# Twenty projection blocks beside a state space scan as three reduced-precision products, with the weights' low parts made by accumulating DMAs

## The chip, the cores and the metric

The kernel runs on one core of a Trainium2 chip. The metric is device time in microseconds (us) of one launch. Five engines work side by side and meet only through semaphores: TensorE (PE, matrix products), VectorE (DVE), ScalarE (ACT), GpSimd (POOL) and SyncE (SP, which only issues DMAs here).

## The reference

Two blocks are computed on 256 tokens of width 1024. The first has two layers (a gated delta rule with attention, then a convolution layer, each followed by a feed-forward part). The second is one hybrid layer, and only its beginning is touched:

```python
def hybrid_layer(x, g_pre_mix, w_in, ...):
    h = rmsnorm(x, g_pre_mix)
    proj = jnp.einsum('bld,dn->bln', h, w_in)          # 1024 -> 6664 columns
    (u_s5, x_conv, b_conv, c_conv, q, k, v, f_logit, gate_logits) = jnp.split(proj, offsets, axis=-1)
    y_a = s5_mixer(u_s5, ...)                          # state space scan, 32 groups of 16 channels, 64 states
    y_b = short_conv_mixer(x_conv, b_conv, c_conv, conv_w)
    y_c = forgetting_attention(q, k, v, f_logit, b_f)
    gates = jax.nn.sigmoid(gate_logits + b_gate)
    merged = sum of gates[i] * (y_i @ w_branch_i)
    x = x + rmsnorm(merged @ w_out, g_post_mix)
    ...                                                # feed-forward part with relu squared
```

`s5_mixer` multiplies u by a complex input matrix, runs a linear recurrence with a complex diagonal over the tokens, multiplies by a complex output matrix and applies gelu and a gate. Everything is float32.

## The kernel before

**Projections.** The product with `w_in` is cut in blocks of 128 output columns. `BLOCKS3` lists 52 of them in order: `in_a` (12 blocks, numbers 0 to 11: u, q, k), `in_v` (4, numbers 12 to 15), `in_b` (12, numbers 16 to 27: the convolution's inputs) and `in_g` (24, numbers 28 to 51: the gates). A plain block is eight float32 matmuls of 128x128 weights on 256 tokens (`feature_block`). ACT copies the finished block out of PSUM (blocks take turns in banks 0 and 1). The gate blocks from `GATE0` = 9 on are made in another way: both operands are split into a high part, rounded to float32r, and a low part, the rest. A block is then 24 float32r matmuls (high by high, low by high, high by low, lines L1456 to L1458). ACT rounds the weights (`gate_round`), DVE subtracts (`gate_split`).

**Weights** come in chunks of three blocks into `ring`, four slots that SP fills as soon as the last block of a slot's chunk before is done.

**The scan** has `S5T` = 16 steps on DVE, each of 128 complex states. Step i waits for its phase table from POOL (`s5_tab`, made by `tables(i)`) and for its input product from PE (`s5_in`, two steps at a time), and then runs L2935 to L2958. POOL's `tables(i)` waits for the rotation of step i-2 (`s5_n`), since it writes that step's buffer. PE takes the states out with `s5_out`, two steps at a time.

**The order beside the scan is written out by hand.** The generator `projections` exists once on PE and once on ACT, and both take `next(filler)` at the same places: four blocks ahead of the scan, then one or two blocks a step (`BESIDE`). PE runs `s5_in(i // 2 + 1)` after the first block of an even step, `s5_out(i // 2 - 1)` at the end of an odd step from 3 on, and `cum_k(i - 13)` in steps 13 to 15. `FORGET` puts small pieces of the attention's forget gate after DVE's steps 7, 9, 11, 14 and 15. `forget(0)` (L2889, L2890) makes `logf_in`, for which ACT waits in its own step 8 (`act.wait_ge(logf_in, 1)`). `forget(3)` (L2908, L2909) reads `cum_k(0)` out of bank 7, so that `cum_k(1)` (L1477) can be written there.

**The gates' input.** ACT rounds `gate_x` (the normalised tokens) to `gate_x_hi` in steps 10 to 13, one of four pairs a step. DVE subtracts after the scan (`gate_x_lo`).

Of the kernel before, what the change touches and what calls it, by code (L numbers as in the profile page):

```python
# [23 lines left out]
F32 = mybir.dt.float32  # L24
# [321 lines left out]

BLOCKS3 = [(_name, _b) for _name, _n in (("in_a", 12), ("in_v", 4), ("in_b", 12), ("in_g", 24)) for _b in range(_n)]
GATE0, GATES = 9, 24
BESIDE = [1 if _i in (2, 5, 8) else 2 for _i in range(S5T)]
FORGET = {7: 0, 9: 1, 11: 2, 14: 3, 15: 4}  # L350

# [13 lines left out]
def build(nc, w, w_mod1, cols_in, rows_in, consts_in, b_out_in, c_bd_in, glu_in, b_in, x_in, ctx_in, out):  # L365
    ctx = ExitStack()
    w = {**w, "mod1": w_mod1}
    with ctx:
# [265 lines left out]
        gates_ready, merged = sem("gates_ready"), sem("merged")  # L634
        gate_x_rounded, gate_x_split = sem("gate_x_rounded"), sem("gate_x_split")
        gate_w_hi, gate_w_lo = sem("gate_w_hi"), sem("gate_w_lo")
        hyb_o_w_hi, hyb_o_w_lo, mix_hi, mix_lo = sem("hyb_o_w_hi"), sem("hyb_o_w_lo"), sem("mix_hi"), sem("mix_lo")
        merged_hi, merged_lo = sem("merged_hi"), sem("merged_lo")
        out2_w_hi, out2_w_lo = sem("out2_w_hi"), sem("out2_w_lo")
# [12 lines left out]
        y_a, y_b = yT[:, 0:4, :], yT[:, 4:8, :]  # L652
        mT, m_lo, m_hi = view(tok_t, 0, KT, T), view(tok_r, 0, KT, T), view(aT_r, 0, KT, T)
        gate_x, gate_x_hi, gate_x_lo = aT[:, :, 0:T], view(aT_r, 0, KT, 2 * T)[:, :, T:2 * T], view(tok_r, 0, KT, T)
        gate_hi = [diag_r[:, 0:D], rowbc_r[:, 0:D], arena_r[:, 14376:14376 + D], z_r[:, 0:D]]
        out2_hi = [arena_r[:, at:at + D] for at in (1024, 4096, 14376, 0, 2048, 3072, 5120, 6144)]
        bT = view(tok_t, 0, 2, 4, P)
# [117 lines left out]
        def _(pe):  # L775
# [659 lines left out]
            def projections():  # L1435

                for name, b in BLOCKS3:
# [11 lines left out]
                    elif name == "in_g" and b >= GATE0:  # L1449
                        w_lo_b, w_hi_b = gate_weights(b, ring_r)  # L1450
                        if b == GATE0:
                            pe.wait_ge(gate_x_split, 4)
                        pe.wait_ge(gate_w_lo, b - GATE0 + 1)
                        for k in range(KT):
                            at = slice(k * P, k * P + P)
                            mm(bank(use)[:, 0:T], w_hi_b[:, at], gate_x_hi[:, k, :], start=(k == 0), stop=False)  # L1456
                            mm(bank(use)[:, 0:T], w_lo_b[:, at], gate_x_hi[:, k, :], start=False, stop=False)  # L1457
                            last = mm(bank(use)[:, 0:T], w_hi_b[:, at], gate_x_lo[:, k, :], start=False, stop=(k == KT - 1))  # L1458
                        filled(last, use)
                    else:  # L1460
                        filled(feature_block(use, slot(c)[:, (b % 3) * D:(b % 3 + 1) * D], lambda k: aT[:, k, 0:T],
                                             fresh=(5,) if (name, b) == ("in_a", 0) else ()), use)
# [153 lines left out]
        def _(act):  # L1616
# [508 lines left out]
            def projections():  # L2125

                for name, b in BLOCKS3:
# [12 lines left out]
                    if name == "in_g" and GATE0 <= b < GATES - 4:  # L2140
                        gate_round(b + 4)
                    yield

            def gate_round(b):

# [1 line left out]
                act.wait_ge(ring_ready[SLOT_OF[c]], 16 * (TURN_OF[c] + 1))  # L2147
                fn(rounded, raw, ACT.Copy).then_inc(gate_w_hi, 1)

            filler = projections()  # L2150
            for _ in range(4):
                next(filler)
            for n, use in enumerate(USE["b_bar"]):
# [13 lines left out]
            for i in range(S5T):  # L2167
# [7 lines left out]
                if i == 8:  # L2175
                    act.wait_ge(logf_in, 1)
                    ch(fn(lf_a, lf_a, ACT.Exp, scale=-1.0))
                    fn(lf_a, lf_a, ACT.Ln, bias=1.0).then_inc(logf_sp, 1)
                if 10 <= i < 14:
                    pair = slice(2 * (i - 10), 2 * (i - 10) + 2)  # L2180
                    fn(gate_x_hi[:, pair, :], gate_x[:, pair, :], ACT.Copy).then_inc(gate_x_rounded, 1)
            next(filler)
            act.wait_ge(s5_state, S5T)
            for b in range(GATE0, GATE0 + 3):
# [69 lines left out]
        def _(dve):  # L2254
# [626 lines left out]

            norm_scale(5)
            norm_evac(5)

            def forget(step):
                if step == 0:
# [202 lines left out]
        def _(pool):  # L3089
# [103 lines left out]
            def tables(i):  # L3193
# [12 lines left out]
                        ch(last)  # L3206
                last.then_inc(s5_tab, 1)

            for i in range(S5T):
                if i >= 2:  # L3210
                    pool.wait_ge(s5_n, i - 1)
                tables(i)
# [115 lines left out]
```

## Time and profile before

| | |
|---|---|
| median of 3 runs | 1311.59 us (1310.51 to 1314.21) |
| the profiled execution | 1312.18 us |
| its span, first to last instruction | 1310.3 us |
| mean granted TensorE clock | 0.985 |
| busy: PE, DVE, ACT, POOL | 1246.6, 908.5, 542.9, 125.2 us |

The profile is one execution. A timeline row is a group of like instructions in order of time: start, length, engine, line, operation, output and inputs, count, and in brackets the idle time before it with what ended it. A float32 matmul stands as two instructions, so 16 of L841 are one block.

### The profile page before, as it was taken

How to read it: one execution, taken by the hardware profiler on the slowest of the kernel's cores; microseconds unless marked ns; L12 is line 12 of the kernel's file. 1: busy time of each engine (PE TensorE's matmuls, PEld its weight loads, DVE VectorE, ACT ScalarE, POOL GpSimd, SP SyncE). 2: the span in 40 equal slices, each digit the busy share in tenths (PEclk: the TensorE clock that was granted, in tenths of full speed). 3: DMA queues.
4: the chain of work that ended last, by engine and by line, in shares of the span. 5: the costliest groups of instructions: out<-in, count | busy, mean ns of one | idle time of the engine just before them, and what ended most of it. 6: DMA issues, size and time to landing. Idle time of an engine off the chain costs nothing. (4 is left out here: it accounts for less than half of the span.)

```text
span 1310.3 us, 19537 instructions
## 1 busy us (share of the span) xinstructions
PE 1246.6 (95%) x7388; PEld 992.4 (76%) x7388; DVE 908.5 (69%) x1557; ACT 542.9 (41%) x907; POOL 125.2 (10%) x165
## 2 busy tenths in 40 slices
PE   4999979999999999999899999899999999899997
PEld 1777646567888887874688888787878987788886
DVE  0548896568777775886777776399977445777776
ACT  2654256446334444014644444302236534544443
POOL 0052021000000002000000000255530000000000
PEclk8999979999999999999999999899999999999999
DMA  9322367865655555422555555124233323555551
GB/s 389 139 86 97 137 267 292 331 269 206 236 192 188 185 182 192 146 80 69 196 206 180 183 187 204 60 86 179 106 134 128 143 104 125 188 192 192 186 182 50
DMA packets 24950, 225.80 MB, mean 172 GB/s; under 512 B 2737, under 2 KB 2865, under 8 KB 4658
## 3 DMA queue, kind: packets, MB, share of 16 engines
q1 hardware_dynamic: 23328, 220.31, 45.9%
q10 hardware_dynamic: 1554, 4.56, 1.0%
q8 instruction: 46, 0.75, 0.2%
q14 instruction: 22, 0.18, 0.0%
HBM read 223.81 MB, written 1.05 MB: 172 GB/s over the span
## 5 line engine op out<-in xcount | busy, mean ns | idle before, releaser
L964 PE MATMUL psum<-aT_r,arena_r 128*128 128x512 f32 x920 | 327.5, 398 | 2.4 <-DVE arena_r L2382 1.9
L2382 DVE TENSOR_TENSOR arena_r<-ring,arena_r 128x1024 fp32r<-128x1024 f32 x188 | 220.4, 1221 | 97.9 <-ACT arena_r L1716 97.9
L965 PE MATMUL psum<-aT_r,arena_r 128*128 128x256 f32 x920 | 258.1, 281 | 0.0
L1716 ACT ACTIVATE arena_r<-ring 128x1024 fp32r<-128x1024 f32 x188 | 186.9, 1051 | 143.4 <-PE psum L999 133.0
L999 PE MATMUL psum<-arena_r 128*128 128x512 f32 x876 | 213.4, 392 | 0.0
L841 PE MATMUL psum<-aT,ring 128*128 128x256 f32 (+1 forms) x896 | 209.7, 393 | 0.0
L964 PEld LDWEIGHTS psum<-aT_r,arena_r 128*128 128x128 f32 x920 | 172.8, 188 | 44.9 <-issue 3.0
L841 PEld LDWEIGHTS psum<-aT,ring 128*128 128x128 f32 x896 | 169.3, 190 | 38.3 <-issue 17.2
L999 PEld LDWEIGHTS psum<-arena_r 128*128 128x128 f32 x876 | 159.5, 188 | 34.7
L965 PEld LDWEIGHTS psum<-aT_r,arena_r 128*128 128x128 f32 x920 | 173.7, 189 | 2.6
L1728 ACT ACTIVATE nrm<-nrm 128x256 f32<-128x256 f32 x76 | 31.8, 418 | 165.1 <-DVE nrm L2400 161.9
L824 PE MATMUL psum<-ring,cond 128*32 128x384 f32 x512 | 53.7, 548 | 20.6 <-DMA consts<-in_consts 12.5
L2770 DVE SCALAR_TENSOR_TENSOR arena<-arena,cols 128x256 f32<-128x256 f32 x120 | 52.8, 482 | 1.9
L824 PEld LDWEIGHTS psum<-ring,cond 128*32 128x32 f32 x512 | 14.9, 118 | 49.0 <-issue 36.9
L2400 DVE TENSOR_REDUCE nrm<-psum 128x256 f32<-128x512 f32 x73 | 49.8, 683 | 0.0
L2417 DVE TENSOR_TENSOR nrm<-nrm 128x256 f32<-128x256 f32 x76 | 32.4, 426 | 22.1 <-ACT nrm L1728 16.6
L2407 DVE TENSOR_REDUCE nrm<-psum 128x256 f32<-128x512 f32 x42 | 29.0, 691 | 20.8 <-PE psum L965 20.8
L2507 DVE SCALAR_TENSOR_TENSOR arena<-arena,cols 128x512 f32<-128x512 f32 (+1 forms) x48 | 35.3, 763 | 1.1
L1457 PE MATMUL psum<-aT_r,ring_r 128*128 128x256 f32 x120 | 33.8, 282 | 0.0
L2425 DVE TENSOR_TENSOR arena_r<-nrm,arena_r 128x256 fp32r<-128x256 f32 x73 | 31.1, 425 | 2.6 <-DVE arena_r L2423 0.2
L3188 POOL MEMSET arena<- 128x24 f32 x1 | 0.1, 121 | 311.6 <-DVE nrm L2309 311.6
L1560 PE MATMUL psum<-yT,ring 128*128 128x256 f32 x128 | 28.9, 379 | 0.0
(551 smaller groups left out, 1894.4 us busy)
## 6 DMA issues: line engine op xcount, KB each, us to landing
ring<-in_w_ffn SPq DMA_DIRECT2D x44, 1536.0 KB, 6.7
ring<-in_w_mod SPq DMA_DIRECT2D x32, 1536.0 KB, 8.6
ring<-in_w_ff SPq DMA_DIRECT2D x32, 1024.0 KB, 4.9
ring<-in_w_in_g SPq DMA_DIRECT2D x8, 1536.0 KB, 6.8
ring<-in_w_conf_i SPq DMA_DIRECT2D x8, 1024.0 KB, 4.8
ring<-in_w_hyb_f SPq DMA_DIRECT2D x4, 1536.0 KB, 6.7
ring<-in_w_in_a SPq DMA_DIRECT2D x4, 1536.0 KB, 6.5
ring<-in_w_in_b SPq DMA_DIRECT2D x4, 1536.0 KB, 6.3
```

Source lines behind the costliest of these rows:

```text
L824: last = mm(mod_banks[run][0][q:q + 32, :], cond[:, at:at + 32], slot(c)[:, k * MOD_C:(k + 1) * MOD_C], start=(m == m0 and k < 4), stop=(m ...
L841: last = mm(bank(use)[:, out_at:out_at + rhs(k).shape[1]], weights[:, k * P:(k + 1) * P], rhs(k), start=(k == 0), stop=(k == KT - 1))
L964: mm(bank(use).rearrange("p (a t) -> p a t", a=2), hi, x_both[:, :, k, :], start=(k == 0), stop=False)
L965: last = mm(bank(use)[:, T:2 * T], lo, x_hi[:, k, :], start=False, stop=(k == KT - 1))
L999: last = mm(Y[:, t, half * 512:half * 512 + 512], act_part, w_part[:, half * 512:half * 512 + 512], start=(isinstance(i, int) and j == 0 a ...
L1457: mm(bank(use)[:, 0:T], w_lo_b[:, at], gate_x_hi[:, k, :], start=False, stop=False)
L1716: fn(out_hi[2] if last_out else w_hi[j % 2][:, at], slot(c)[:, at], ACT.Copy).then_inc(split_hi, 1)
L2382: tt(lo, slot(c)[:, at], hi.bitcast(F32), ALU.subtract).then_inc(split_ready, 1)
L2400: summed = v.reduce_sum(g_sum[:, j % 2, :], bank(gate).rearrange("p (a t) -> p t a", a=2), axis=AXX)
L2417: tt(h_tmp, sg[:, j % 2, :], u_sum if parts == 3 else sg[:, j % 2, :], ALU.mult).then_inc(h_step, 1)
L2507: last = stt(cv[:, b, 0:n, :], cin[:, b, 0:n, k:k + T], taps[:, b, k:k + 1], cv[:, b, 0:n, :], ALU.mult, ALU.add)
L2770: last = stt(cc[:, c, :], cu[:, c, k:k + T], dww[:, c, k:k + 1], cc[:, c, :], ALU.mult, ALU.add)
```

## The change

Blocks 4 to 11 and 16 to 27 (`PARTED`, twenty of them) are made of three float32r products, as the late gate blocks are.

- ACT rounds `gate_x` ahead of the first block and no longer in steps 10 to 13. DVE makes a second low part of it, `scan_x_lo`, ahead of the scan. The later `gate_x_lo` stays.
- For each block ACT first writes the negated weights, rounded, to one of five buffers (`scan_negate`, five blocks ahead). POOL then issues a DMA that adds the weights to that buffer (`scan_add`), which leaves the weights less their rounded value there: the low part. When that DMA has landed, ACT rounds the weights in place in the ring (`scan_round`, two blocks ahead).
- ACT's two instructions follow the copy of a block in `projections`, after its `yield`. POOL issues the DMAs in its loop over the steps, ahead of the wait for `s5_n` and of `tables(i)`: five ahead of `tables(1)`, then 2, 1, 0, 1, 2, 2, 2, 2, 2, 1 ahead of `tables(2)` to `tables(11)`.
- PE waits for `scan_hi` ahead of each of the blocks.

```diff
+PARTED = [_n for _n, (_name, _b) in enumerate(BLOCKS3) if _name == "in_b" or _name == "in_a" and _b >= 4]
+PARTED_AHEAD = 5
...
+        scan_x_lo = view(decay_r, 0, KT, T)
+        scan_lo = [ybuf_r[:, 0:D], ybuf_r[:, D:2 * D], o_r[:, 0:D], arena_r[:, 12328:12328 + D], arena_r[:, 13352:13352 + D]]
...
+                    elif BLOCKS3.index((name, b)) in PARTED:
+                        s = PARTED.index(BLOCKS3.index((name, b)))
+                        w_hi_s, w_lo_s = scan_weights(s, ring_r), scan_lo[s % PARTED_AHEAD]
+                        if s == 0:
+                            pe.wait_ge(scan_x_split, 4)
+                        pe.wait_ge(scan_hi, s + 1)
+                        for k in range(KT):
+                            at = slice(k * P, k * P + P)
+                            mm(bank(use)[:, 0:T], w_hi_s[:, at], gate_x_hi[:, k, :], start=(k == 0), stop=False)
+                            mm(bank(use)[:, 0:T], w_lo_s[:, at], gate_x_hi[:, k, :], start=False, stop=False)
+                            last = mm(bank(use)[:, 0:T], w_hi_s[:, at], scan_x_lo[:, k, :], start=False, stop=(k == KT - 1))
+                        filled(last, use)
...
                     yield
+                    n = BLOCKS3.index((name, b))
+                    if n + 2 in PARTED:
+                        scan_round(PARTED.index(n + 2))
+                    if n + PARTED_AHEAD in PARTED:
+                        scan_negate(PARTED.index(n + PARTED_AHEAD))
+
+            def scan_negate(s):
+
+                name, b = BLOCKS3[PARTED[s]]
+                c = FIRST[name] + b // 3
+                act.wait_ge(ring_ready[SLOT_OF[c]], 16 * (TURN_OF[c] + 1))
+                fn(scan_lo[s % PARTED_AHEAD], scan_weights(s, ring), ACT.Copy, scale=-1.0).then_inc(scan_neg, 1)
+
+            def scan_round(s):
+
+                act.wait_ge(scan_low[s % PARTED_AHEAD], 16 * (s // PARTED_AHEAD + 1))
+                fn(scan_weights(s, ring_r), scan_weights(s, ring), ACT.Copy).then_inc(scan_hi, 1)
...
+            for kp in range(4):
+                pair = slice(2 * kp, 2 * kp + 2)
+                wait_read(act, USE["norm5"][kp])
+                fn(gate_x_hi[:, pair, :], gate_x[:, pair, :], ACT.Copy).then_inc(gate_x_rounded, 1)
             filler = projections()
+            scan_negate(0)
...
-                if 10 <= i < 14:
-                    pair = slice(2 * (i - 10), 2 * (i - 10) + 2)
-                    fn(gate_x_hi[:, pair, :], gate_x[:, pair, :], ACT.Copy).then_inc(gate_x_rounded, 1)
...
             norm_evac(5)
+            for kp in range(4):
+                pair = slice(2 * kp, 2 * kp + 2)
+                dve.wait_ge(gate_x_rounded, kp + 1)
+                tt(scan_x_lo[:, pair, :], gate_x[:, pair, :], gate_x_hi[:, pair, :].bitcast(F32),
+                   ALU.subtract).then_inc(scan_x_split, 1)
...
+            def scan_add(s):
+
+                pool.wait_ge(scan_neg, s + 1)
+                gp.dma_start(scan_lo[s % PARTED_AHEAD], scan_weights(s, ring),
+                             accum_op=ALU.add).then_inc(scan_low[s % PARTED_AHEAD], 16)
+
+            s = 0
             for i in range(S5T):
+                while s < len(PARTED) and i >= 1 and PARTED[s] <= PARTED_AHEAD + 2 * i + 1:
+                    scan_add(s)
+                    s += 1
                 if i >= 2:
                     pool.wait_ge(s5_n, i - 1)
                 tables(i)
```

## Rows read from the trace of the kernel before

**Rows 1.** Windows, steps 1 to 13: us, busy PE, PEld, DVE, ACT, POOL.

```profile
858.30:956.30 98.00, 98.00 (x484) 78.42 (x483) 93.76 (x139) 21.14 (x40) 54.80 (x79) 1.00 0.39 139
```

**Rows 2.** Waits from 833 to 1000 us, all engines: the first of DVE.

```profile
DVE diag L2935 <- PE psum L1487: 16.7, 1, 16.7
```

**Rows 3.** Timeline of DVE: starts of steps 1, 2, 7, 9, 15; forget(0), forget(4).

```profile
858.29 0.69 DVE L2935 TENSOR_TENSOR diag<-psum,rowbc 128x512 f32<-128x512 f32 x1
...
865.67 0.69 DVE L2935 TENSOR_TENSOR diag<-psum,rowbc 128x512 f32<-128x512 f32 x1
...
902.80 0.68 DVE L2935 TENSOR_TENSOR diag<-psum,rowbc 128x512 f32<-128x512 f32 x1
...
910.53 0.17 DVE L2890 SCALAR_TENSOR_TENSOR arena<-arena 128x16 f32<-128x16 f32 x1
...
917.64 0.69 DVE L2935 TENSOR_TENSOR diag<-psum,rowbc 128x512 f32<-128x512 f32 x1
...
965.17 0.69 DVE L2935 TENSOR_TENSOR diag<-psum,rowbc 128x512 f32<-128x512 f32 x1
...
970.72 0.69 DVE L2908 TENSOR_TENSOR o<-psum,arena 128x512 f32<-128x512 f32 x1
```

**Rows 4.** Timeline of PE: s5_in(1), two plain blocks, cum_k(1), cum_k(2), one three-product block.

```profile
855.18 1.13 PE L1487 MATMUL psum<-arena,tok 32*128 32x256 f32 x8
...
900.70 7.07 PE L841 MATMUL psum<-aT,ring 128*128 128x256 f32 x32
...
964.80 1.10 PE L1477 MATMUL psum<-arena,consts 128*128 128x512 f32 x2 [1.23 <-DVE ybuf L2909]
...
973.72 1.12 PE L1477 MATMUL psum<-arena,consts 128*128 128x512 f32 x2
...
991.92 0.39 PE L1456 MATMUL psum<-aT_r,diag_r 128*128 128x256 f32 x1
...
994.77 0.28 PE L1458 MATMUL psum<-tok_r,diag_r 128*128 128x256 f32 x1
```

**Rows 5.** Timeline of ACT: norm, block copies 2 and 15, b_bar, step 8, glu_open(0), weight rounding.

```profile
833.47 1.94 ACT L1652 ACTIVATE aT<-psum,nshift,ngain 128x256 f32<-128x256 f32 x4 [2.13 <-PE psum L798]
...
845.39 0.38 ACT L2131 ACTIVATE arena<-psum 128x256 f32<-128x256 f32 x1 [3.07 <-PE psum L841]
...
849.28 1.08 ACT L2155 ACTIVATE tok<-psum 128x512 f32<-128x512 f32 x2
...
900.90 0.39 ACT L2134 ACTIVATE arena<-psum 128x260 f32<-128x260 f32 x1 [4.38 <-PE psum L1446]
...
912.85 1.28 ACT L2177 ACT_TABLE_LOAD   x1
...
915.66 0.21 ACT L2178 ACTIVATE arena<-arena 128x16 f32<-128x16 f32 x1
...
917.99 1.28 ACT L2165 ACT_TABLE_LOAD   x1
...
978.71 1.05 ACT L2148 ACTIVATE diag_r<-ring 128x1024 fp32r<-128x1024 f32 x1
979.66 1.05 ACT L2148 ACTIVATE rowbc_r<-ring 128x1024 fp32r<-128x1024 f32 x1
```

**Rows 6.** Timeline of POOL: first and last of tables(9), and its longest instruction.

```profile
908.22 0.62 POOL L3201 TENSOR_TENSOR yT<-arena 128x256 f32<-128x256 f32 x1 [3.00 <-DVE nrm L2948]
...
911.84 0.72 POOL L3204 TENSOR_TENSOR rowbc<-yT 128x256 f32<-128x256 f32 x1
...
988.49 2.17 POOL L3218 TENSOR_TENSOR ybuf<-ybuf,consts 128x512 f32<-128x512 f32 x1 [11.57 <-DVE ybuf L2909]
```

**Rows 7.** Timeline of SP: one DMA issue.

```profile
784.07 0.34 SPq L722 DMA_DIRECT2D ring<-in_w_ffn  x1
```

**Rows 8.** Issues of DMAs by line: count, KB each, median us to landing.

```profile
ring<-in_w_hyb_t SPq DMA_DIRECT2D x4, 1296.0 KB, 10.0
...
tok<-in_c_bd ACTq DMA_DIRECT2D x1, 512.0 KB, 3.7
```

More of the change, by code:

```diff
@@ L636, in build @@
         gate_w_hi, gate_w_lo = sem("gate_w_hi"), sem("gate_w_lo")
+        scan_x_split, scan_neg, scan_hi = sem("scan_x_split"), sem("scan_neg"), sem("scan_hi")
+        scan_low = [sem(f"scan_low{b}") for b in range(PARTED_AHEAD)]
         hyb_o_w_hi, hyb_o_w_lo, mix_hi, mix_lo = sem("hyb_o_w_hi"), sem("hyb_o_w_lo"), sem("mix_hi"), sem("mix_lo")
@@ L654, in build, with scan_weights @@
         gate_x, gate_x_hi, gate_x_lo = aT[:, :, 0:T], view(aT_r, 0, KT, 2 * T)[:, :, T:2 * T], view(tok_r, 0, KT, T)
+        scan_x_lo = view(decay_r, 0, KT, T)
+        scan_lo = [ybuf_r[:, 0:D], ybuf_r[:, D:2 * D], o_r[:, 0:D], arena_r[:, 12328:12328 + D], arena_r[:, 13352:13352 + D]]
+        def scan_weights(s, t):
+            name, b = BLOCKS3[PARTED[s]]
+            return out_weights(FIRST[name] + b // 3, b % 3, t)
         gate_hi = [diag_r[:, 0:D], rowbc_r[:, 0:D], arena_r[:, 14376:14376 + D], z_r[:, 0:D]]
@@ L2142, in projections @@
                     yield
+                    n = BLOCKS3.index((name, b))
[4 more added lines that the diff above has]
+            def scan_negate(s):
+                name, b = BLOCKS3[PARTED[s]]
+                c = FIRST[name] + b // 3
[4 more added lines that the diff above has]
+                fn(scan_weights(s, ring_r), scan_weights(s, ring), ACT.Copy).then_inc(scan_hi, 1)
             def gate_round(b):
```

## The prediction

> **What bounds the kernel now.** I read the stretch around the change, not the page's shares. The busy times of the scan's stretch [rows 1] show PE busy for all 98 us of the scan's steps 1 to 13, and DVE for 93.76 of them: a reader who stops there takes PE for the bound. The waits and the timelines say otherwise. DVE sits idle 16.7 us until the first input product comes [rows 2], and from then on never waits: steps 1 and 2 start 7.38 us apart [rows 3], and so it goes on to step 15. PE, though never idle before, meets DVE at the end: `cum_k(1)`, at 964.80, is preceded by 1.23 us of idling that DVE's `forget(3)` ends [rows 4]. This piece runs when step 14 is over. So a PE that is 12 us early at 963.6 waits 13 us there. What sets the time of this stretch is the start of the scan and the sixteen steps of DVE. After `cum_k(1)` PE has its plain blocks back to back, and `cum_k(2)` comes at 973.72, when DVE has freed its bank by 970.72 + 0.69 + 0.69 = about 972 [rows 3, 4]: a PE that resumes late stays late by the whole amount. The forecast is therefore one number: by how much DVE's step 14 ends later or earlier.
>
> **PE's part.** Two plain blocks take 7.07 us, one 3.5. Of a three-product block the 24th matmul starts 994.77 - 991.92 = 2.85 after the first, so one takes about 2.9 [rows 4]. Twenty blocks save 20 x 0.6 = 12 us, all of it ahead of `cum_k(1)`. Worth on the path: 0.
>
> **DVE's part.** Four subtractions of 128x512, about 0.6 us each, 2.5 us, are added ahead of step 0. The 16.7 us of idle [rows 2] hide them; without this cover they would cost 2.5.
>
> **ACT's part.** Four roundings move from steps 10 to 13 to the start. There they take 2.5 us beside PE's first block of 3.5, and ACT idles 3.07 us ahead of a block's copy [rows 5], so they cost nothing. Twenty negations and twenty roundings of 128x1024 are new, 979.66 - 978.71 = 0.95 us each in a row [rows 5], 38 us on top of 21.14 in 98 [rows 1]. The sum fits. What is behind them matters: PE waits for the rounding, POOL for the negation, DVE for POOL's table. POOL's DMAs stand ahead of `tables(i)`, so **DVE's step i now waits for ACT**, which in turn waits for PE and DVE. This chain did not exist.
>
> **POOL's part.** The trace has no DMA issued by POOL. One issue occupies it for c: at least the 0.34 us that an issue takes on SP's queue [rows 7], at most the 2.17 of POOL's longest instruction here [rows 6]. I take 1.0, nearer to its table instructions (0.62 to 0.79). For the landing L of 512 KB the rows give 3.7 us for as many bytes, and 10.0 for the slowest weight load [rows 8]; an addition reads two operands, so I take 5. The Trainium skill ("DMA: Bandwidth & Descriptors", "Anatomy of one DMA") fits 2.0 us and bytes over 436 GB/s to a DMA from GpSimd, an estimate of 3.2 us here; no run here shows it, and it would leave the sum as it is.
>
> **The coupling, step by step** (times before; `tables(i)` takes 911.84 + 0.72 - 908.22 = 4.3 us, [rows 6]):
> - Start. ACT is through its norm at 833.47 + 1.94 = 835.4, then 4 x 0.6 and the first negation: 838.8. Block 4's rounding stands behind the copy of block 2 (845.39 + 0.38) [rows 5]. With c + L = 6 the sum has landed at 844.8: no wait. Up to 8.0 the slack ahead of the fourth copy (845.39 + 3.5 = 848.9) still hides it. Beyond that the b_bar copy at 849.28, and with it the scan's start, slips one for one.
> - `tables(1)` stands behind five DMAs; the fifth negation follows the b_bar copy (850.36) and a rounding: 852.3. Add c and 4.3: 857.6, against step 1 at 858.29 [rows 3]. No wait.
> - `tables(2)` stands behind block 5's copy. PE: block 4 starts 3.5 ahead of `s5_in(1)` at 855.18 [rows 4], 851.6; with 2.9 + 1.1 + 2.9 block 5 ends at 858.5; copy, rounding, negation 860.8; c and 4.3: 866.1 against 865.67: slip 0.4.
> - `tables(7)` stands behind block 15's copy, 900.90 [rows 5], now eight blocks x 0.6 = 4.8 earlier, 896.1. With copy 0.4, 1.9, c and 4.3: 903.7 against 902.80: 0.9.
> - `tables(9)`, the large one. ACT waits in its step 8 for `logf_in`, which DVE makes behind step 7: 910.53 + 0.17 = 910.7 [rows 3]. Before, ACT came there at 912.85 [rows 5] and did not wait. Now it comes some 6.6 us earlier (11 blocks x 0.6) and stands still until 910.7. Then exp and ln with their table loads, 915.87 - 912.85 = 3.0: 913.7. Then block 20's rounding and block 23's negation, 1.9: 915.6. Copy of block 19, 0.4; `glu_open(0)` with its table load, 1.7: 917.7. Block 21's rounding and block 24's negation: 919.6. POOL's second DMA of this step: 920.6. `tables(9)`: 924.9. Before, step 9 started at 917.64 [rows 3]. **Slip 7.3.**
> - Steps 10 on: block 26's negation comes near 924, DMAs 25 and 26 end at 927, `tables(10)` at 931.3, against step 10 at 924.9 + 7.4 = 932.3. No more waits at c = 1.0; at 2.17 some 1.3 more.
>
> **The sum.** 7.3, plus the 0.9 that moved step 7 and with it `logf_in`, is 8.2. Against it stands a relief. A step beside a table takes 7.38 us, step 15 without one 970.72 - 965.17 = 5.55 [rows 3]: 1.8 us a step are lost to POOL running beside DVE. Tables that come later meet other instructions, or a waiting DVE. I take off 0.5 for one or two steps that lie better. So +7.7, or 8 rounded. The profiled execution took 1312.18, 1.9 more than its span and 0.6 more than the median; 1312.2 + 8 = **1320 us**. With c = 0.34: two issues less 0.66 each in `tables(9)` are not both on the path (the first hides behind ACT), so 1319. With c = 2.17: 1.2 in `tables(9)`, 1.2 in `tables(7)`, 1.3 in step 10, so about 1324.
>
> **The rivals.**
> 1. *The forecast*, ACT's wait for `logf_in` behind which the negations queue: 1316 to 1324, chance 0.55.
> 2. *The DMA lands late.* If c + L is over 8.0 the scan starts late by the rest, and PE waits for each rounding. With L = 10.0 and c = 1.0: 3 us at the start, about 2 more at `tables(2)` and `tables(7)`, where ACT also waits for landings ahead of the negation, and the 7.7: 1325. With both at their upper ends 8 at least, and ACT late in most steps, 1335 and over. For it: an addition of two operands in a DMA is not in the trace. Against: 3.7 us for as many bytes [rows 8]. Chance 0.2.
> 3. *Nothing is seen.* The slips are eaten by relief: 0.5 us of the 1.8 in each of thirteen steps is 6.5, leaving 1 to 2. For it: the added DMAs do push the tables later. Against: before, the middle of `tables(9)` (908.22 to 912.56) already lay beside the next step's reads of PSUM, from 910.7 on [rows 3, 6], where POOL takes no operand from DVE's side. 1311 to 1315, chance 0.15.
> 4. *Faster*: relief again, but in most steps and nearly all of it. The point from which it decides is 8 + 4 = 12 us over thirteen steps, 0.9 each; at 1.3 each it is 17 - 8 = 9 us, 1303. The Trainium skill ("SBUF — State Buffer", "Who interferes with whom") says that DVE with two SBUF inputs and a reading GpSimd exclude one another for whole instructions. By that rule what a step loses depends on which instructions meet, and by it a table moved behind DVE's reads of PSUM meets more of them, not fewer. The same end has the reading of PE as the bound, 12 us off, 1300; the 1.23 us of idling [rows 4] speaks against it. Both together 0.1.
>
> **Numbers.** A measurement of this kernel tells about 0.3%, 4 us, from no change. Slower: rivals 1 and 2, 0.75. Same 0.15, faster 0.1. The range leaves out rival 4 and the worst of rival 2: 1311 to 1334. The forecast's own range is 1316 to 1324.
>
> **What would show it.** In the profile after: blocks of L841's kind replaced by 24 products, 2.9 us each, and PE idle in the scan by some 20 us, most of it in front of `cum_k(1)`. DVE idle in front of L2935 (its table) for 7 us in one place, at step 9, and under 2 us at steps 2 and 7. ACT idle in front of the exp of `logf`, released by DVE's L2890. POOL's issues of about 1 us and landings of about 5. If instead the scan starts later than 851.7, rival 2 holds; if DVE's steps are 6 to 6.5 us long, rivals 3 or 4. The forecast is wrong if ACT's negations of blocks 23 and 24 are not behind that wait, or if DVE gains more in its steps than it loses at step 9.

## The result, and the profile after

The changed kernel takes 1333.85 us (median of 4 runs, 1328.81 to 1335.17), the kernel before 1311.75 beside it: ratio 1.0151, 95% interval 1.0128 to 1.0173, slower by some 22 us. The forecast was slower too, but by 8. All ratios below rest on executions at the usual granted clock; one of e5's ten, of 1714.85 us at a granted clock of 0.691, is in none of them.

The profiled execution took 1335.16 us with a span of 1333.4, 23.1 more than before. Not all of that belongs to the change. The windows of the changed kernel (us, busy time of PE, PEld, DVE, ACT and POOL, granted clock, DMA share, GB/s), first the stretch of [rows 1], then one from a stage whose code is the same:

```profile
858.30:956.30 98.00, 82.61 (x566) 72.17 (x566) 87.18 (x119) 46.42 (x63) 66.74 (x86) 0.93 0.82 209
...
600.00:650.00 50.00, 47.82 (x154) 25.69 (x153) 34.05 (x92) 27.26 (x55) 0.00 (x0) 0.90 0.35 127
```

In the second row the granted clock averages 0.90, where the profile of before had 1.00 in the same window, with the same code. Such dips ahead of the change add up: ACT's norm ahead of the projections, at 833.47 before [rows 5], comes at 837.29, 3.8 us later, when nothing of the change has run yet, and the scan begins at 855.53 instead of 851.67, 3.9 later. In the profiles of the twelve experiments below, with the same code up to that norm, the norm comes anywhere from 830.87 to 840.14 and the scan from 849.14 to 858.86; in all fourteen profiles the scan starts 18.1 to 18.8 us behind the norm. Single profiles are therefore compared from the scan's start on: from there to the end of the span it is 1310.3 - 851.67 = 458.6 us before and 1333.4 - 855.53 = 477.9 after, **19.2 us more**, near the 22 between the medians.

Within the scan, the first term is a wait. DVE's timeline after, the end of step 7, the end of step 8 and the beginning of step 9 (start, duration, idle ahead of it and what ended that):

```profile
922.57 0.17 DVE L2937 SCALAR_TENSOR_TENSOR arena<-arena 128x16 f32<-128x16 f32 x1
...
927.90 0.42 DVE L3005 SCALAR_TENSOR_TENSOR z<-nrm 128x256 f32<-128x256 f32 x1
935.57 0.69 DVE L2982 TENSOR_TENSOR diag<-psum,rowbc 128x512 f32<-128x512 f32 x1 [7.25 <-POOL rowbc L3251]
```

ACT and then POOL in the same stretch:

```profile
922.78 0.22 ACT L2222 ACTIVATE arena<-arena 128x16 f32<-128x16 f32 x1 [1.30 <-DVE arena L2937]
...
924.43 1.04 ACT L2182 ACTIVATE ring_r<-ring 128x1024 fp32r<-128x1024 f32 x1
925.38 1.04 ACT L2177 ACTIVATE ybuf_r<-ring 128x1024 fp32r<-128x1024 f32 x1
...
926.71 1.28 ACT L2210 ACT_TABLE_LOAD   x1
928.00 0.39 ACT L2210 ACTIVATE yT<-psum 128x256 f32<-128x256 f32 x1
928.28 1.05 ACT L2182 ACTIVATE ring_r<-ring 128x1024 fp32r<-128x1024 f32 x1
929.23 1.05 ACT L2177 ACTIVATE ybuf_r<-ring 128x1024 fp32r<-128x1024 f32 x1
```

```profile
926.72 0.87 POOL L3259 DMA_DIRECT2D ybuf_r<-ring  x1 [4.22 <-ACT ybuf_r L2177]
930.58 0.86 POOL L3259 DMA_DIRECT2D ybuf_r<-ring  x1 [2.98 <-ACT ybuf_r L2177]
931.14 0.95 POOL L3248 TENSOR_TENSOR yT<-arena 128x256 f32<-128x256 f32 x1
...
934.81 0.72 POOL L3251 TENSOR_TENSOR rowbc<-yT 128x256 f32<-128x256 f32 x1
```

This is the chain that the prediction wrote out, link by link: exp and ln behind `logf_in`, a rounding and a negation, a block's copy, `glu_open(0)` with its table load, again a rounding and a negation, and only then POOL's addition and `tables(9)`. It is the only place in the scan where DVE waits for a table.

The second and larger term shows as no wait at all. The groups of DVE's instructions by line from the scan's start to `cum_k(1)`, after (busy us, mean ns of one):

```profile
L2991 DVE TENSOR_TENSOR_SCAN nrm<-arena,nrm 128x256 f32<-128x256 f32 x30 | 26.6, 927 | 0.5
L2994 DVE TENSOR_TENSOR nrm<-nrm,rowbc 128x512 f32<-128x512 f32 x15 | 13.9, 928 | 0.5
...
L2995 DVE TENSOR_TENSOR nrm<-nrm,rowbc 128x512 f32<-128x512 f32 x15 | 12.0, 803 | 0.0
...
L2982 DVE TENSOR_TENSOR diag<-psum,rowbc 128x512 f32<-128x512 f32 x16 | 11.0, 688 | 20.7 <-PE psum L1510 12.7 <-POOL rowbc L3251 7.3
L2983 DVE TENSOR_TENSOR diag<-psum,rowbc 128x512 f32<-128x512 f32 x16 | 10.9, 678 | 0.0
```

Before, the same groups:

```profile
L2944 DVE TENSOR_TENSOR_SCAN nrm<-arena,nrm 128x256 f32<-128x256 f32 x30 | 19.1, 678 | 0.5
...
L2935 DVE TENSOR_TENSOR diag<-psum,rowbc 128x512 f32<-128x512 f32 x16 | 11.0, 688 | 17.6 <-PE psum L1487 16.7
...
L2947 DVE TENSOR_TENSOR nrm<-nrm,rowbc 128x512 f32<-128x512 f32 x15 | 10.4, 692 | 0.5
```

The second of the last products had 685 ns, the second product out of PSUM 679. The scans and the last products have become slower, the products out of PSUM have not. In busy time up to `cum_k(1)`, the scans, the last two products and the first addition (L2940 before, L2987 after) grew by 7.5, 3.5, 1.7 and 3.2 us, while the two state operations that end a step fell by 5.4 and the second addition by 0.6. That makes some 10 us, with the wait of 7.25 some 17: the whole growth of this stretch lies in that wait and in the lengths of DVE's own instructions. DVE and POOL therefore meet not only through semaphores, as the section on the chip has it: POOL's tables lengthen DVE's instructions without one. What the tables do depends on which instructions they lie beside; e10 below shows it.

The third term, behind the scan, is the clock. PE's timeline after, and the window around `cum_k(1)`:

```profile
985.26 2.04 PE L1500 MATMUL psum<-arena,consts 128*128 128x512 f32 x2 [8.41 <-DVE ybuf L2956]
987.09 8.24 PE L852 MATMUL psum<-aT,ring 128*128 128x256 f32 x32
```

```profile
980.00:988.00 8.00, 2.74 (x5) 1.56 (x6) 7.74 (x16) 0.00 (x0) 1.65 (x1) 0.50 0.28 117
```

PE stands idle for 8.41 us ahead of `cum_k(1)`; the granted clock of the window is 0.50, that is 1.2 GHz; `cum_k(1)` takes 2.04 us instead of 1.10 and the two plain blocks behind it 8.24 instead of 7.07 [rows 4]. From `cum_k(1)` to `cum_k(2)` it is 10.99 us instead of 8.92.

**The sum of the 19.2.** The 113.13 us from the scan's start to `cum_k(1)` have become 129.73, 16.6 more. Step 8, with the wait of 7.25 in it, grew from 7.0 to 12.9, 5.9; the other steps of that stretch grew by 10.7 together, with no wait. From `cum_k(1)` to the end it is 345.5 before and 348.1 after, 2.6 more, of which 2.07 lie ahead of `cum_k(2)`; the other 0.5 was not followed.

### The profile page after: what moved, and what is told of

It reads as the page before. It is cut to its first block and busy times, and to the rows that moved or that the text cites. A ratio compares the mean times of both kernels' runs of the same rounds, so it can differ in the third digit from the quotient of the medians.

```text
span 1333.4 us, 19935 instructions
## 1 busy us (share of the span) xinstructions
PE 1250.3 (94%) x7548; PEld 1001.5 (75%) x7548; DVE 921.0 (69%) x1561; ACT 580.4 (44%) x947; POOL 149.0 (11%) x185
## 5 line engine op out<-in xcount | busy, mean ns | idle before, releaser
L852 PE MATMUL psum<-aT,ring 128*128 128x256 f32 (+1 forms) x576 | 138.8, 401 | 0.0
L852 PEld LDWEIGHTS psum<-aT,ring 128*128 128x128 f32 x576 | 110.3, 193 | 28.0 <-issue 14.5
L1479 PE MATMUL psum<-aT_r,ring_r 128*128 128x256 f32 x160 | 48.3, 302 | 4.4 <-ACT ring_r L2182 4.4
L1481 PE MATMUL psum<-decay_r,ring_r 128*128 128x256 f32 x160 | 46.6, 291 | 0.0
L1479 PEld LDWEIGHTS psum<-aT_r,ring_r 128*128 128x128 f32 x160 | 31.9, 200 | 8.7 <-issue 8.6
```

Source lines behind the costliest of these rows:

```text
L852: last = mm(bank(use)[:, out_at:out_at + rhs(k).shape[1]], weights[:, k * P:(k + 1) * P], rhs(k), start=(k == 0), stop=(k == KT - 1))
L1479: mm(bank(use)[:, 0:T], w_hi_s[:, at], gate_x_hi[:, k, :], start=(k == 0), stop=False)
L1481: last = mm(bank(use)[:, 0:T], w_hi_s[:, at], scan_x_lo[:, k, :], start=False, stop=(k == KT - 1))
```

## Experiments

All times are compared with runs of the kernel before on the same chip (its medians there: 1313.9 to 1314.8 us). The columns from the third on are of the profiled execution, in us; they leave out what happened before the scan.

| kernel | median, ratio [95%] | scan's start to cum_k(1) | PE idle ahead of it | cum_k(1) to end |
|---|---|---|---|---|
| before | 1311.75 | 113.1 | 1.23 | 345.5 |
| changed | 1333.85, 1.0151 [1.0128, 1.0173] | 129.7 | 8.41 | 348.1 |
| e1_late_logf | 1331.76, 1.0134 [1.0117, 1.0151] | 127.1 | 8.30 | 347.9 |
| e2_adds_behind | 1323.01, 1.0074 [1.0052, 1.0096] | 118.7 | 4.67 | 348.7 |
| e3_wait_no_dma | 1326.78, 1.0103 [1.0071, 1.0134] | 122.2 | 8.43 | 348.6 |
| e4_no_pool | 1317.56, 1.0019 [1.0003, 1.0034] | 113.5 | 7.90 | 347.6 |
| e5_before_pool_dmas | 1315.21, 1.0009 [0.9998, 1.0020] | 113.2 | 1.29 | 345.4 |
| e7_both_fill | 1320.21, 1.0043 [1.0021, 1.0065] | 124.4 | 2.81 | 341.0 |
| e8_fill_no_pool | 1312.17, 0.9980 [0.9961, 0.9999] | 113.5 | 1.66 | 341.6 |
| e9_two_behind_fill | 1332.61, 1.0148 [1.0125, 1.0171] | 142.5 | none | 339.4 |
| e10_tables_late | 1325.86, 1.0090 [1.0063, 1.0117] | 121.1 | 9.22 | 347.4 |
| e11_negate_first | 1330.86, 1.0136 [1.0105, 1.0167] | 126.3 | 6.28 | 348.1 |
| e12_first_behind_fill2 | 1315.47, 1.0015 [1.0000, 1.0031] | 117.4 | 1.43 | 343.9 |
| e13_first_fill2 | 1323.76, 1.0073 [1.0051, 1.0095] | 122.0 | 5.41 | 346.4 |

### Is PE's saving worth anything, and what does it cost? e4

```diff
             def scan_add(s):
-                pool.wait_ge(scan_neg, s + 1)
-                gp.dma_start(scan_lo[s % PARTED_AHEAD], scan_weights(s, ring), accum_op=ALU.add)...
+                pass
             def scan_round(s):
-                act.wait_ge(scan_low[s % PARTED_AHEAD], 16 * (s // PARTED_AHEAD + 1))
```

> POOL neither waits nor issues, so its tables are as before; PE makes the twenty blocks of three products and ACT negates and rounds. The low parts are left as the negated rounded weights. If the twelve us that PE saves are worth nothing because DVE's scan sets the end (my step), 1311 to 1314, with 13 us of PE idle in front of cum_k(1) and the clock lower behind it (up to 2 us). If PE is the bound: 1300.

Every instruction that PE and ACT have in the change is there, but POOL is as before, and ACT waits for no landing. The buffers hold the negated weights where the low parts should be, so the kernel does the work without giving the reference's result; the same holds for e3 and e8. The steps are those of before to 0.1 us each (sum 113.5 against 113.1), and PE's 12 us buy nothing: PE's timeline, e4:

```profile
967.34 2.04 PE L1500 MATMUL psum<-arena,consts 128*128 128x512 f32 x2 [7.90 <-DVE ybuf L2955]
```

So ACT's forty copies and DVE's four subtractions are hidden, as forecast, and the saving turns into idle time; the stretch behind it is 347.6 - 345.5 = 2.1 us longer, 1.6 of it ahead of `cum_k(2)`, at a granted clock of 0.50 at first. The time, 1317.56, is 3.6 over the expected 1311 to 1314, and PE's idle is 7.9 instead of 13. Nearly all the rest of the change's loss comes in by POOL, or by ACT's waits for landings, which e4 leaves out as well.

### The waits, the additions, or the place of the tables? e3, e5, e10, e1

e3 keeps POOL's wait for each negation and leaves the addition out (so POOL's code is tables and waits alone). ACT's wait for the landing goes with it:

```diff
             def scan_round(s):
-                act.wait_ge(scan_low[s % PARTED_AHEAD], 16 * (s // PARTED_AHEAD + 1))
...
                 pool.wait_ge(scan_neg, s + 1)
-                gp.dma_start(scan_lo[s % PARTED_AHEAD], scan_weights(s, ring), accum_op=ALU.add)...
```

> POOL waits for each negation as in the changed kernel but issues no DMA, and ACT rounds without waiting for a landing. The low parts are left as the negated rounded weights. Theory B: the waits alone keep most of the loss, about 1328 (the 0.86 us of each issue is gone). Rival D: near before, 1312 to 1318, because what disturbs DVE is the DMA.

122.2 us to `cum_k(1)`: POOL's waits alone cost 8.7 over e4, the additions and ACT's waits for their landings another 7.5 (129.7). The time, 1326.78, is near the 1328 of theory B. The 7.5 could be the price of the additions themselves, as traffic or as time on POOL. e5 tests this from the other side, in the kernel before. Its additions all read one tile of constants, go to buffers that nobody reads, and wait for no negation; only the main lines of the edit are shown:

```diff
+            def scan_add(s):
+                gp.dma_start(scan_lo[s % PARTED_AHEAD], consts[:, 0:D], accum_op=ALU.add)...
             for i in range(S5T):
+                while s < len(PARTED) and i >= 1 and PARTED[s] <= PARTED_AHEAD + 2 * i + 1:
+                    scan_add(s)
+                    s += 1
                 if i >= 2:
                     pool.wait_ge(s5_n, i - 1)
                 tables(i)
```

> The kernel before with only the transfers added: 20 accumulating DMAs of 512 KB, issued by POOL at the places in its loop where the change issues them, into buffers that nobody reads (the values are of no use), without any wait for ACT; they wait only for the landing of the one that used the same buffer. Theory 1 (the issue on POOL and the tables it pushes together take DVE's cycles, apart from any wait for ACT): the stretch from the scan's start to cum_k(1), 113.1 us before, grows by 4 to 8 us, and the time comes to 1319 to 1323 against 1314.8 of before. Theory 2 (only the waits for ACT's negations hurt, the transfers ride beside them): growth under 1.5 us, 1314 to 1316.5. POOL DMA issue 0.85 to 1.0 us and landing 6 to 9 us in both.

Theory 2 held: ratio 1.0009, and 113.2 us to `cum_k(1)`. Twenty additions of 512 KB, 10.5 MB, each issued by POOL at the change's own place, cost nothing, although they landed slower than the change's (medians 11.4 to 14.0 us against 6.7 to 8.5). POOL and then DVE in e5, over one step:

```profile
876.52 0.62 POOL L3211 TENSOR_TENSOR yT<-arena 128x256 f32<-128x256 f32 x1 [3.00 <-DVE nrm L2958]
...
880.12 0.79 POOL L3214 TENSOR_TENSOR rowbc<-yT 128x256 f32<-128x256 f32 x1
880.85 0.87 POOL L3225 DMA_DIRECT2D decay_r<-consts  x1
883.91 0.61 POOL L3211 TENSOR_TENSOR yT<-arena 128x256 f32<-128x256 f32 x1 [2.19 <-DVE nrm L2958]
```

```profile
876.54 0.87 DVE L2966 TENSOR_TENSOR arena<-nrm 128x256 f32<-128x256 f32 x1
877.34 0.83 DVE L2968 SCALAR_TENSOR_TENSOR arena<-nrm 128x256 f32<-128x256 f32 x1
878.27 0.69 DVE L2945 TENSOR_TENSOR diag<-psum,rowbc 128x512 f32<-128x512 f32 x1
878.87 0.68 DVE L2946 TENSOR_TENSOR diag<-psum,rowbc 128x512 f32<-128x512 f32 x1
879.66 0.66 DVE L2950 TENSOR_TENSOR nrm<-diag 128x256 f32<-128x256 f32 x1
880.24 0.94 DVE L2951 TENSOR_TENSOR nrm<-diag 128x256 f32<-128x256 f32 x1
881.22 1.27 DVE L2954 TENSOR_TENSOR_SCAN nrm<-arena,nrm 128x256 f32<-128x256 f32 x2
882.53 0.69 DVE L2957 TENSOR_TENSOR nrm<-nrm,rowbc 128x512 f32<-128x512 f32 x1
```

The reader is to see the phase. DVE's last product of a step releases POOL, so that the tables begin together with the next instruction of DVE, every time; the issue falls into POOL's own idle time (3.00 us, of which 2.19 is left, and 1.30 where there are two issues). Of the tables' 4.3 us the 1.4 beside the two products out of PSUM slow nothing down. In the change the wait for ACT stands in front of the tables, and this phase is lost. e10 takes the phase away and nothing else, in the kernel before: `tables(i)` starts when step i-1 has read its input out of PSUM.

```diff
                 if i >= 2:
                     pool.wait_ge(s5_n, i - 1)
+                    wait_read(pool, USE["s5_u"][i - 1])
                 tables(i)
```

> The kernel before with one wait more: for each pass from the third on, POOL begins the tables only when DVE's second product of the step before has been done, some 2.3 us after the point at which it began before. No transfer, no wait for ACT, no other work. Theory 1 (what DVE loses in the changed kernel is that POOL's table instructions now run beside its two additions, the scan and the last products, instead of beside the state operations and the products out of PSUM): DVE's steps grow by 0.5 to 2 us each without any wait for a table, the scan's start to cum_k(1) grows from 113.1 us to 119 to 128, and the time to 1319 to 1327 against 1314. Theory 2 (a table that comes 2 us later harms nothing as long as it is there in time; the growth is from the added transfers and copies): under 1 us more, 1313 to 1316.

Theory 1 held: 1325.86 us, ratio 1.009, and 121.1 us to `cum_k(1)`, 8.0 more, without a transfer, a copy or a wait for a table. One step of e10, DVE and then POOL:

```profile
872.55 0.69 DVE L2935 TENSOR_TENSOR diag<-psum,rowbc 128x512 f32<-128x512 f32 x1
873.16 0.68 DVE L2936 TENSOR_TENSOR diag<-psum,rowbc 128x512 f32<-128x512 f32 x1
873.95 0.42 DVE L2940 TENSOR_TENSOR nrm<-diag 128x256 f32<-128x256 f32 x1
874.29 0.84 DVE L2941 TENSOR_TENSOR nrm<-diag 128x256 f32<-128x256 f32 x1
875.16 2.06 DVE L2944 TENSOR_TENSOR_SCAN nrm<-arena,nrm 128x256 f32<-128x256 f32 x2
...
878.11 1.10 DVE L2948 TENSOR_TENSOR nrm<-nrm,rowbc 128x512 f32<-128x512 f32 x1
879.31 0.76 DVE L2956 TENSOR_TENSOR arena<-nrm 128x256 f32<-128x256 f32 x1
```

```profile
873.97 0.87 POOL L3201 TENSOR_TENSOR yT<-arena 128x256 f32<-128x256 f32 x1 [2.13 <-DVE diag L2936]
...
878.74 1.05 POOL L3204 TENSOR_TENSOR rowbc<-yT 128x256 f32<-128x256 f32 x1
```

The tables start 1.42 us behind the step's start (873.97 - 872.55), where before they start 1.75 ahead of it (863.92 against 865.67): 3.2 us later in the step. The products out of PSUM keep their 0.69 and 0.68, but now nothing runs beside them; the whole table lies beside instructions with two operands in SBUF, and the two scans take 2.06 us instead of 1.27, the last product 1.10 instead of 0.68. The state operations win a part of it back, 0.76 and 0.41 instead of 0.88 and 0.83. A step grows from 7.4 to 8.0. The same is seen in the changed kernel, and worse, where one of POOL's DMAs is issued directly ahead of a late table (DVE, then POOL):

```profile
856.93 1.85 DVE L2987 TENSOR_TENSOR nrm<-diag 128x256 f32<-128x256 f32 x1
858.71 0.94 DVE L2988 TENSOR_TENSOR nrm<-diag 128x256 f32<-128x256 f32 x1
859.68 1.96 DVE L2991 TENSOR_TENSOR_SCAN nrm<-arena,nrm 128x256 f32<-128x256 f32 x2
```

```profile
856.41 0.85 POOL L3259 DMA_DIRECT2D arena_r<-ring  x1 [3.74 <-ACT arena_r L2177]
856.97 0.95 POOL L3248 TENSOR_TENSOR yT<-arena 128x256 f32<-128x256 f32 x1
857.56 0.93 POOL L3249 TENSOR_TENSOR yT<-arena 128x256 f32<-128x256 f32 x1
```

Here DVE's first addition of the step takes 1.85 us instead of 0.42: it ends at 858.78, 0.3 us behind POOL's second table instruction. The step takes 8.8 instead of 6.6. The Trainium skill ("SBUF — State Buffer", "Who interferes with whom") says that a DVE instruction with two inputs in SBUF and a GpSimd instruction that reads SBUF lock one another out for a whole instruction, and that one with a single SBUF input goes free. These rows agree with both halves: the two products out of PSUM have means of 688 and 679 ns before and in e10, with tables beside them and without, and the scans 678 ns before and 1042 in e10.

e1 takes away the one visible wait, by moving ACT's exp and ln of logf one step later:

```diff
-                if i == 8:
+                if i == 9:
                     act.wait_ge(logf_in, 1)
```

> Against the changed kernel (about 1333 us; before about 1312). ACT takes the exp and ln of the forget gate at the end of its step 9 instead of step 8, so the negations of blocks 23 and 24 no longer queue behind DVE's forget(0). Theory A (ACT's wait for logf_in costs 7.25 us of DVE idle at step 9): that idle goes and about 6 us with it, 1327. Theory B (most of the slip is POOL's tables colliding with DVE because they run later and back to back): the idle goes but the steps of 8.5 to 9.5 us stay, again 1327 to 1330, and the steps' busy time stays about 10 us over that of before. Rival C (the landing of the DMAs holds everything): no change, 1333.

The wait of 7.25 is gone (what is left are 1.50 at step 7 and 0.62 at step 9), but only 2.7 us with it (129.7 to 127.1), and the ratio hardly moves: 1331.76 is over what either theory allowed (1327, and 1327 to 1330), though the longer steps that theory B expected are there (8.7 to 9.8 us for steps 7 to 11). While DVE waited at step 9 it lost nothing to POOL: step 8 without its wait took 12.9 - 7.25 = 5.6 us, where 7.0 is usual. Once the wait is gone the collisions come back.

### What makes POOL late? e2, e11, e9

e2 issues each addition one pass later. The bound is the only edit:

```diff
-                while s < len(PARTED) and i >= 1 and PARTED[s] <= PARTED_AHEAD + 2 * i + 1:
+                while s < len(PARTED) and i >= 1 and PARTED[s] <= PARTED_AHEAD + 2 * i + -1:
```

> Every accumulating DMA is issued one pass of POOL's loop later, so that no table stands behind a negation that ACT has not made yet. The same DMAs, the same ACT and PE work. Theory B (waiting for ACT shifts the tables, and shifted tables collide): tables lie where they lay before, both the 7.25 us of idle and the 10 us of longer steps go, 1312 to 1315. Rival D (the DMAs themselves, descriptors written by GpSimd or traffic in SBUF, slow DVE): the idle goes, the longer steps stay, 1320 to 1325.

Half of the loss goes: ratio 1.0074. By the time, 1323.01, this is rival D's range and not theory B's 1312 to 1315, but rival D's cause, the transfers themselves, is not it: the same twenty are issued, and steps 0 to 5 are back at 6.6 and 7.4, and no table is waited for. Steps 7 to 11 still take up to 10.2, because POOL still waits there for ACT, up to 5.1 us, and ACT in turn for landings. e11 cuts this last link by a swap of two calls:

```diff
+                    if n + PARTED_AHEAD in PARTED:
+                        scan_negate(PARTED.index(n + PARTED_AHEAD))
                     if n + 2 in PARTED:
                         scan_round(PARTED.index(n + 2))
-                    if n + PARTED_AHEAD in PARTED:
-                        scan_negate(PARTED.index(n + PARTED_AHEAD))
```

> The changed kernel with two ACT operations in the other order: after each block the negation of five blocks ahead comes first, and only then the rounding that waits for a transfer. Theory 1 (POOL's waits for negations are in part ACT's own waits for landings, 5 and 3 us, and its 1.05 us roundings, passed on): POOL's waits for negations fall from 36.6 us by 8 or more, and the time from 1333.9 to 1325 to 1330. Theory 2 (the negation waits for PE to free its buffer, so nothing is gained): 1332 to 1335.

The waits of e11, POOL's for negations:

```profile
POOL ybuf_r L3259 <- ACT ybuf_r L2177: 11.9, 6, 3.9
...
POOL arena_r L3259 <- ACT arena_r L2177: 11.1, 5, 3.7
POOL o_r L3259 <- ACT o_r L2177: 7.1, 2, 4.5
```

They sum to 30.1 us against 16.9 + 13.3 + 6.4 = 36.6 in the change, 6.5 less, a little under the 8 that the first theory asked; 3.4 us come out of it (129.7 to 126.3), and DVE's wait for the table of step 9 is still 6.32. The time, 1330.86, falls by 3 as well, to between the ranges of the two theories, but the interval (1.0105 to 1.0167) overlaps the change's, so by the time alone this is no more than likely. e9 goes the other way, additions two passes late, with e1's edit and with three more gate blocks beside the scan (two guards in DVE's `gate_split` calls, which follow from the smaller number of late gate blocks, are not shown):

```diff
-GATE0, GATES = 9, 24
+GATE0, GATES = 12, 24
-BESIDE = [1 if _i in (2, 5, 8) else 2 for _i in range(S5T)]
+BESIDE = [2] * S5T
-                if i == 8:
+                if i == 9:
-                while s < len(PARTED) and i >= 1 and PARTED[s] <= PARTED_AHEAD + 2 * i + 1:
+                while s < len(PARTED) and i >= 1 and PARTED[s] <= PARTED_AHEAD + 2 * i + -3:
```

> As e7, but the additions two passes later than in the change, not one. Theory 1 (POOL waits on ACT's negations because they come just in time; another pass of slack takes the waits away): POOL's waits for the negations under 1 us each, the 16 steps of the scan within 2 us of those of before, but PE waits for the low parts instead, so the time is near that of e7, 1313 to 1320. Theory 2 (POOL's waits stay, since ACT's negations are held by the buffers coming free from PE and not by time): steps 7 to 11 stay 2 us longer each and the time is that of e7 or worse, 1316 to 1324.

Both theories missed: 1332.61. The waits of e9:

```profile
PE psum L1479 <- ACT ring_r L2182: 22.2, 7, 7.4
DVE arena L2940 <- ACT arena L2223: 15.4, 1, 15.4
```

What is late enough for POOL's place is too late for PE, which now stands 22 us in front of rounded weights (ACT in turn 23.6 us in front of landings in `arena_r`), and DVE waits 15.4 us for the ln that e1's edit put behind them.

### Can PE's 12 us be used? e8, e7, e13, e12

e8 is e4 with the three gate blocks moved (the first two edits of e9). The edit does more than move them. `GATE0` is also the first gate block made of three products, so the three blocks that come into the scan are plain ones, 3 x 3.54 = 10.6 us, while what leaves the stretch behind are three three-product blocks, 3 x 2.9 = 8.7: L1468 runs 120 times in e4 and 96 in e8. PE has 2 us more to do in all. The expectations of e7 and e8 took off 10.6:

> The changed kernel without POOL's waits and additions (low parts are the negated rounded weights, so the projections aren't the reference's, as in e4), with the three gate blocks moved into the scan. It shows what PE's freed time is worth where nothing disturbs the scan. Theory 1: e4 had 7.9 us of idle before cum_k(1) and a slow cum_k(1); 10.6 us of blocks fill it, cum_k(1) comes 2.7 us later, 10.6 us behind it go and about 2 us of clock come back: 1317.6 - 10.6 + 2.7 - 2, about 1307.5 (1304 to 1311), under the kernel before. Theory 2 (DVE, ACT or the evictions of the three blocks lengthen the scan by as much as they save): 1314 to 1318.

The idle is filled (1.66 left), the clock holds, and `cum_k(1)` comes at 113.5 as before. But of the 8.7 us that leave the stretch behind it only 3.9 are gained on the kernel before (345.5 to 341.6; 6.0 on e4). PE now meets another wait there, 2.4 us in front of L796 for DVE, and the granted clock is 0.91 in the window of 20 us around that wait, 1.00 before and in e4. The rest of the difference was not followed. The time, 1312.17, lies between the two expected ranges. Ratio 0.998: the gain is 0.2%, in a kernel that leaves out the additions altogether.

e7 is the same with the additions, one pass late, and e1's edit:

> The changed kernel with the additions one pass later (e2), ACT's exponential and logarithm of logf at pass 9 (e1), and with PE's freed time used: three gate blocks (10.6 us of TensorE at 3.54 each) moved from behind the scan to passes 2, 5 and 8 of it. Theory 1 (PE's saving was worth nothing only because PE then waits at cum_k(1), and the idle costs clock): PE had 4.7 us of idle there in e2, so cum_k(1) comes about 6 us later than in e2, the 10.6 us behind it are gone and some 2 us of clock come back: 1323.0 - 10.6 + 6 - 2, about 1316 (1312 to 1320), with no idle before cum_k(1). Theory 2 (what is behind the scan is bound by something other than PE): 1325 to 1330.

1320.21, 4 over the expected 1316 and just outside its range: `ln` came late again and DVE waited 7.0 us for it; e1's edit harms here. So it was left out in the last two. They move two gate blocks (7.1 us into the scan, 5.8 out of the stretch behind) and negate first; e13 leaves the additions at their places, e12 issues them one pass late. e13 has e11's edit and the first two here, e12 all three:

```diff
-GATE0, GATES = 9, 24
+GATE0, GATES = 11, 24
-BESIDE = [1 if _i in (2, 5, 8) else 2 for _i in range(S5T)]
+BESIDE = [1 if _i == 2 else 2 for _i in range(S5T)]
-                while s < len(PARTED) and i >= 1 and PARTED[s] <= PARTED_AHEAD + 2 * i + 1:
+                while s < len(PARTED) and i >= 1 and PARTED[s] <= PARTED_AHEAD + 2 * i + -1:
```

> As e12, but the additions at the change's own places. Blocks moved into the scan bring PE forward against the passes, so that each addition comes later counted in blocks than in the changed kernel already. Theory 1: POOL's waits and the collisions stay at the first seven passes (the steps 0 to 6 together 4 to 6 us longer than before), after that they are less; the scan's start to cum_k(1) about 122 to 125 and the time 1316 to 1321. Theory 2 (the waits are as in the change, with the 7 us wait for a table at step 9): 1322 to 1328.

> The changed kernel with the negation first (e11), the additions one pass later (e2), and two gate blocks (7.1 us) moved from behind the scan to passes 5 and 8, which fits the idle time that PE has before cum_k(1). Theory 1: e2 takes 118.7 us from the scan's start to cum_k(1) with 4.7 us of PE idle, so two blocks make that about 120.5 and take 7.1 us and the clock's loss of 2 to 3 us from the 348.7 behind it: 1323 - 9.5 + 2, about 1315.5, and less by what the order saves: 1312 to 1316.5, level with the kernel before. Theory 2 (with less slack in blocks PE comes to wait for the low parts, as in e9): 1318 to 1326.

e13 comes to 1323.76, over the 1316 to 1321 of theory 1 and inside the 1322 to 1328 of theory 2, whose 7 us wait at step 9 is not there (0.81): the first seven steps cost 5.8 more than before and the stretch to `cum_k(1)` is 122.0, both as theory 1 had it, but PE still idles 5.41 ahead of `cum_k(1)`. e12 is the best form of the change that was found: PE idles 1.43 ahead of `cum_k(1)`, which takes 1.10, and the stretch behind is 1.6 shorter than before (345.5 to 343.9); the scan's is 4.3 longer. Ratio 1.0015 [1.0000, 1.0031]: level with the kernel before, not better. No version beat the kernel before with the reference's result intact.

## Why the prediction was wrong by 14 us

**What held.** PE's 12 us are worth nothing on the path (e4), DVE's subtractions and ACT's copies are hidden (e4: steps unchanged), DVE and not PE bounds the scan. The chain to `tables(9)` is the one written out: from `logf_in` (922.57 + 0.17 = 922.74) to the table's end it was to take 14.2 us and took 12.8; DVE was to be there 6.9 after `logf_in` and was there 5.6 after; the wait forecast at 7.3 is 7.25. That the two agree to 0.05 is luck: the two times it is the difference of were each 1.3 to 1.4 too long. One reason is that ACT loads its first table ahead of the wait for `logf_in` (920.20), not behind it, so that exp and ln are through 1.8 us after `logf_in` (924.53) instead of 3.0. ACT's wait there is 1.30 us, not the 4.4 that the prediction's times give. c was put at 1.0 and is 0.85 to 1.01, 1.16 where one issue follows another. The slips of 0.4 and 0.9 at steps 2 and 7 were not there as waits.

**The step that failed** is in the sum: "Tables that come later meet other instructions, or a waiting DVE. I take off 0.5 for one or two steps that lie better." The term has the wrong sign and a twentieth of the measured size: without step 8 the steps grew by 10.7 us. The step had the number that should have warned (1.8 us lost per step to POOL) but treated it as something to be won back. It did not ask why the loss was only 1.8. The rows of before answer it: the tables start in the same instant as DVE's state operations, and a third of their length lies beside DVE's reads of PSUM. A delay can only move that third to a worse place. e10 shows the price of this alone, 8.0 us for tables that start 3.2 us later in each step, without any part of the change. Rival 4 cited the rule and drew the right conclusion from it ("meets more of them, not fewer"), but no time was worked out from that conclusion, and it moved neither the sum nor a chance.

**The waits were looked for in the wrong form.** Every slip was worked out as "table ready, against step's start", so that a table in time cost nothing. By that measure POOL's wait for ACT was free at steps 1 to 8. In fact before step 8 had begun 8.2 us were lost (922.68 - 855.53 = 67.2 from the scan's start, 59.0 before) with no table late.

**L was low.** Put at 5, the landings of the 512 KB additions have medians of 6.7, 6.9 and 8.5 us. The estimate of 3.2 us from the Trainium skill ("DMA: Bandwidth & Descriptors", "Anatomy of one DMA") is further off. The longer landing delays ACT's roundings (5.3 and 3.2 us of waits), and ACT's negations stand behind these; e11 puts that at some 3 us. The scan's start, where rival 2 expected the price, was not touched: it is 3.86 us late where the norm ahead of it is 3.82 late (837.29 against 833.47). The time of 1333.85 is near rival 2's 1335, but that price was put on a late start and on PE's waits for roundings (4.4 us here, hidden), and neither made it.

**A term was missing.** PE's idle in front of `cum_k(1)` was foreseen as harmless, but the granted clock is 0.50 behind it: the stretch to the end is longer by 2.6 us here and by 2.1 in e4, most of it ahead of `cum_k(2)`. The idle itself is 8.41 us and not most of 20: another 15.4 lie in PE's waits for DVE and ACT inside the scan.

Together: +5.9 (step 8) + 10.7 + 2.6 = 19.2, against +7.3 + 0.9 - 0.5 = 7.7 in the forecast. What remains open: how the 10.7 divides between the plain phase shift (e10), the issues that now stand back to back with tables, and later tables that no longer fit; e3 puts 8.7 on POOL's waits, the wait for a table at step 9 (6.60 there) included, and 7.5 on the additions and ACT's waits for their landings, which no run takes apart. That the medians differ by 22 and the profiles by 19.2 from the scan's start on was not followed up; the four executions of the changed kernel alone range over 6.4 us.

## What to carry to other kernels

Two engines whose instructions hold each other up have a phase, and a tuned loop may live by it: before adding a wait to the one with slack, look at which instructions of the other its work lies beside, not only at when its result is due. Put new work of such an engine behind its regular work, into its idle time (e5: free), and put no wait for a third engine in front of the regular work (e3: 8.7 us). And time saved on an engine that is off the path is not neutral if the idle it leaves lowers its clock; either fill it (e12) or leave the engine busy.

## What the hardware showed unexpectedly

- Twenty accumulating transfers of 512 KB issued by POOL, landing in 11 to 14 us, did not slow DVE (e5: 113.2 against 113.1 us for the stretch, and no group of the scan's own instructions with a mean over 2 ns longer).
- The scan instruction is lengthened beside POOL's tables as the elementwise ones are: two of 128x256 take 1.27 us alone (before) and 1.96 to 2.06 beside tables (after, e10).
- When POOL's DMA issue and its first table instructions follow each other without a gap, a DVE addition of 0.42 us took 1.85 and 1.98 (steps 0 and 1 of the changed kernel), longer than any one of POOL's instructions there.
- `cum_k(1)` took 1.10 us where PE had idled 1.23 to 1.66 us ahead of it, and 2.04 or 2.05 where it had idled 2.81 to 9.22 us, in all the kernels of the table that show an idle.
